# One addition of two weight slabs on VectorE is placed earlier in the order of its engine

## The reference

```
h = rmsnorm(x, g_ffn)
z = dwconv3(h @ w_up)                    # w_up: 1024 x 5632; three taps over the positions
z_gate, z_val = split(z)                 # 2816 each
x = x + (silu(z_gate) * z_val) @ w_down
```

## Time and profile before

| | |
|---|---|
| time, three runs | 1087.05, 1088.1, 1088.28 us (median 1088.1) |
| profiled execution | 1088.28 us |
| its span, first to last instruction | 1086.5 us |
| mean granted clock of TensorE | 0.996 |
| busy: PE, DVE, ACT, POOL | 1072.4, 643.6, 556.8, 629.0 us |
| `add_s2`, 16 of them | 35.1 + 12.8 us |
| POOL's `low` | 2.4 to 2.7 us each |

### The profile page before, as it was taken

One profiled execution on the slowest core, in us unless ns is written; L12 is line 12 of the kernel. 1 busy time (PEld: TensorE's weight loads), 2 busy tenths in 40 slices (PEclk: granted clock), 3 DMA queues, 4 the chain that ended last, 5 costly groups with the idle time before them and its releaser, 6 DMA issues.

```text
span 1086.5 us, 18356 instructions
## 1 busy us (share of the span) xinstructions
PE 1072.4 (99%) x6492; PEld 943.9 (87%) x6492; DVE 643.6 (59%) x938; ACT 556.8 (51%) x772; POOL 629.0 (58%) x298
## 2 busy tenths in 40 slices
PE   9999999999999999999999999999999999999997
PEld 7788888888889989998878888888879998899987
DVE  5725755667197731776636368556744786147764
ACT  7835444545356623675548244445434575257651
POOL 6334334344789848995534332434458895789940
PEclk9999999999999999999999999999999999999999
DMA  8332123232866446762522222222338763767412
GB/s 304 96 97 79 59 78 99 78 115 78 213 176 173 119 140 169 173 142 95 179 84 80 79 78 71 89 93 78 116 114 220 158 149 98 194 155 188 115 48 78
DMA packets 40549, 134.35 MB, mean 124 GB/s; under 512 B 4752, under 2 KB 7568, under 8 KB 40464
## 3 DMA queue, kind: packets, MB, share of 16 engines
q1 hardware_dynamic: 32848, 107.03, 30.5%
q0 software_dynamic: 6912, 25.17, 13.5%
q10 hardware_dynamic: 704, 1.07, 0.3%
HBM read 122.76 MB, written 2.10 MB: 115 GB/s over the span
## 4 chain that ended last, share of the span: by engine, by line
PE 95%; DVE 3%; DMA 1%; ACT 0%; POOL 0%; SPq 0%; issue 0%; DVEq 0%
PE acc L1482 18%; PE acc L1483 17%; PE acc L1484 17%; PE acc L1796 9%; PE acc L1799 9%; PE acc L1798 9%; PE acc L1608 3%; PE acc L1609 3%; PE acc L1610 3%; DVE second_s L1311 2%; PE sides L1578 1%; PE sides L1680 1%; PE sides L1696 1%; DMA x<-xT 1%; PE sides L1686 1%; PE sides L1659 1%
## 5 line engine op out<-in xcount | busy, mean ns | idle before, releaser
L465 POOL TENSOR_TENSOR w_lo<-w_raw,w_hi 128x1024 fp32r<-128x1024 f32 x108 | 261.4, 2426 | 334.9 <-ACT w_hi L522 329.0
L455 POOL TENSOR_TENSOR w_lo<-w_raw,w_hi 128x1024 fp32r<-128x1024 f32 x72 | 183.9, 2581 | 56.7 <-ACT w_hi L805 44.0
L1482 PE MATMUL acc<-feat_hi,w_hi 128*128 128x512 f32 (+1 forms) x496 | 190.1, 383 | 1.6 <-DVE x L1227 1.5
L1483 PE MATMUL acc<-feat_lo,w_hi 128*128 128x512 f32 (+1 forms) x496 | 189.7, 382 | 0.0
L1484 PE MATMUL acc<-feat_hi,w_lo 128*128 128x512 f32 (+1 forms) x496 | 189.6, 382 | 0.0
L522 ACT ACTIVATE w_hi<-w_raw 128x1024 fp32r<-128x1024 f32 x102 | 107.8, 1063 | 139.8 <-PE acc L1484 103.4
L1796 PE MATMUL acc<-xg_hi,w_hi 128*128 128x256 f32 x512 | 146.6, 286 | 4.6 <-DVE sides L1333 4.6
L1799 PE MATMUL acc<-xg_hi,w_lo 128*128 128x256 f32 x512 | 146.2, 286 | 0.0
L1798 PE MATMUL acc<-xg_lo,w_hi 128*128 128x256 f32 x512 | 146.2, 286 | 0.0
L1482 PE MATMUL acc<-xg_hi,w_hi 128*128 128x512 f32 x352 | 139.6, 397 | 0.0
L1483 PE MATMUL acc<-xg_lo,w_hi 128*128 128x512 f32 x352 | 137.1, 389 | 0.0
(11 more groups left out here) (179 smaller groups left out, 2164.6 us busy)
## 6 DMA issues: line engine op xcount, KB each, us to landing
w_raw<-slabs SPq DMA_DIRECT2D x166, 512.0 KB, 3.5
w_raw<-slabs POOLq DMA_DIRECT2D x16, 512.0 KB, 5.5
arena<-slabs SPq DMA_DIRECT2D x16, 512.0 KB, 4.8
arena<-slabs POOLq DMA_DIRECT2D x16, 512.0 KB, 5.4
mixer_sb<-slabs SPq DMA_DIRECT2D x8, 512.0 KB, 5.0
w_raw<-mixer_sb POOLq DMA_DIRECT2D x8, 512.0 KB, 4.6
mixer_sb<-second_s POOLq DMA_DIRECT2D x8, 512.0 KB, 4.5
outT<-arena SPq DMA_DIRECT2D x7, 256.0 KB, 2.2
```

Of the source, the lines that this page charges most:

```text
L455: pool.tensor_tensor(w_lo[:, w], source, w_hi[:, w].bitcast(F32), ALU.subtract).then_inc(lo_done, 1)
L465: pool.tensor_tensor(w_lo[:, w], w_raw[:, w], w_hi[:, w].bitcast(F32), ALU.subtract).then_inc(lo_done, 1)
L1482: pe.matmul(out, wh, ah, start=first, stop=False)
L1483: pe.matmul(out, wh, al, start=False, stop=False)
```

## The change

`convolve` takes a function more and calls it between the taps of tile 2 and gate 0. In quads 1 and 2 of each part that function is `add_s2(p, s + 1)`, which stood behind `convolve` and c11. In quad 0 there is no `convolve` ahead, and `add_s2(p, 1)` now stands before c11. `add_s2(p, 0)` stays where it was, and no other engine's order changes.

```diff
-                def convolve(p, s):
+                def convolve(p, s, between):
 
                     add_c12(p, s)
                     scale(p, s, 0)
...
                     taps(p, s, 2)
+                    between()
                     gate(p, s, 0)
                     taps(p, s, 3)
                     quad_low(p, s, 0)
...
                 def quad_step(p, s):
                     if s:
-                        convolve(p, s - 1)
+                        convolve(p, s - 1, (lambda: add_s2(p, s + 1)) if s < KP - 1 else (lambda: None))
+                    else:
+                        add_s2(p, 1)
                     add_c11(p, s)
-                    if s < KP - 1:
-                        add_s2(p, s + 1)
                     add_c22(p, s)
                     add_c21(p, s)
                     scale(p, s, 1)
...
-                    convolve(p, KP - 1)
+                    convolve(p, KP - 1, lambda: None)
```

## The result

The changed kernel took 1096.54 us (median of five, 1095.78 to 1098.7) against 1088.15 for the kernel before: ratio 1.0076, 95% interval 1.0057 to 1.0095. So it is slower by 8.4 us; 1097.2 was forecast, +8.9. The profiled execution took 1098.84 us with a span of 1097.0, at the upper end of what the kernel shows. Lines behind the edit are one higher than before (products are L1797, L1799, L1800). In all that follows "quad 1's add" is the add that stands in quad 1 and makes S2 for quad 2, and so on.

The account below looks back on a forecast made before the run. TensorE, busy 99% of the span, was taken as the bound, so only its stops could be won back. Two vanishing stops (-8.05) and four new ones (4.70 + 4.18 + 2 x 4.02) gave +8.9 on 1088.28: 1097.2 us, range 1087.5 to 1106.

Parts of the forecast that it names:

- The stops that vanish: Part 0's first quad, both layers: TensorE's stops of 2.69 and 2.18 us vanish, with slowed products behind them, -8.05 us.
- The rule for a waiting add: A waiting DVE add gets in only where POOL's next instruction begins later than 0.14 us before the last one's end.
- limit for the A11 low: Quads 1 and 2: A11's low must end before -0.59 us from the quad's TensorE start, or the add is held.
- the four adds of the forecast: A11's ends: part 0 quad 1 +0.34 and -0.18 (layers 0, 1), quad 2 -0.69 (served); part 1 quad 2 -0.34; others held.
- Part 1, quad 2: Add held to S4's end in both layers, TensorE 2.43 us late plus 1.59 for the clock: 4.02 us each, +8.04.
- Part 0: Quad 1's add held in both layers, costing 4.70 and 4.18 us; quad 2's served by a margin of 0.10 us, 0.
- The clock: Behind each of the four new TensorE stops a lowered clock lengthens the next product, 1.59 us each.
- The sum: Whole kernel: -8.05 + 4.70 + 4.18 + 2 x 4.02 = +8.9 us, giving 1097.2 us.
- D: Rival: all adds get in at the next low's end, in a tight chain too; 1080.2 us, chance 0.20.
- B: Rival: part 0's quad 2 add is held too, 2 x 4.0 us more; 1105.2 us, chance 0.17.
- C: Rival: only quad 1 of part 0 is held, part 1 keeps its gaps; +0.85, 1089.1 us, chance 0.18.
- E: Rival: as the forecast, but a stop of 2.4 us doesn't lower the clock; 1094.0 us, chance 0.07.

Follow-up runs that it names:

- The gap in quads 1 and 2: Changed kernel, with POOL waiting for its own A22 low before the S3 low in quads 1 and 2 only: 1080.13 us, ratio 0.9927 to the kernel before.
- a gap at the boundary: Changed kernel, with POOL waiting for its own A22 low before the S3 low in every quad: 1080.58 us, ratio 0.9939 to the kernel before.
- a gap one boundary earlier: Changed kernel, with POOL waiting for its own S2 low before the A22 low: 1081.38 us, ratio 0.9945 to the kernel before.
- no second input: Changed kernel, with the add replaced by a same-size reduction reading S1 alone (result not the layer's): 1080.56 us, ratio 0.9925 to the kernel before.
- The run with quad 0 alone: Kernel before, with only quad 0's add moved before c11, all other adds left in place: 1086.87 us, ratio 0.9993.
- The run with the gap in part 1 alone: Changed kernel, with POOL waiting for its own A22 low before the S3 low in part 1 only: 1091.54 us, ratio 1.0039 to the kernel before.

## Why the prediction was right

**The stops that vanish.** Right, both, in every execution with quad 0's move. The gap in quads 1 and 2 takes away all others, and the kernel is 7.7 us below that before where 8.05 was counted.

**The rule for a waiting add.** Right in kind, and shown by changing one thing at a time: a gap at the boundary, a gap one boundary earlier, no second input (with the operation changed along with it). An overlap of 0.12 in layer 1 let the add in, 0.34 in layer 0 did not. The number 0.14 is another matter: it is the lead with which DVE starts before a low's recorded end, and the prediction took it for the limit of the overlap too. The run with quad 0 alone served an add at 0.18, so if one limit holds for lows and DMA issues alike, it lies between 0.18 and 0.30. The forecast's limit for the A11 low, -0.59, was worked out with 0.14; with 0.18 to 0.30 it would be -0.55 to -0.43, and the four adds of the forecast (+0.34 and -0.18, -0.69, -0.34) stay on the side where they were put.

**Part 1, quad 2.** The adds and the stops are right to a few hundredths of a us. Forecast from the quad's start: A22 +6.56, S3 +8.92, S4's end +13.96, TensorE at +16.83. Measured: +6.53, +8.90, +13.97, +16.84. With the products behind them the two stops cost 5.1 us in one execution and 6.5 in the other, where 8.04 was forecast: the clock, below, makes the difference. The run with the gap in part 1 alone prices them at 4 to 5 us.

**Part 0.** Right in kind, uncertain in place. I had quad 1 held in both layers and quad 2 served, by 0.10 us. One execution shows just that; in the other, quad 2 is held in both layers and quad 1 in layer 0 only. Two causes can be read. In quad 1, layer 1, the A11 low ended at -0.31 (forecast -0.18), later than the limit of -0.59, and yet the add was served. The limit was wrong for this quad: it came from quad 3, where ACT's high for S3 is ready at +8.79, and here it was ready at +9.08, so the S3 low began only at +9.15 and A22, begun at +6.57, was just early enough. In the other execution the high was as late, but A22 began at +6.88, and the add was held. And quad 2 follows from quad 1. Where the clock stays up behind quad 1's stop, quad 2 starts sooner than the 7.35 us behind TensorE's resumption that I used (5.86, at 326.59 to 332.45), and A11's low, at +0.77, misses the limit; where quad 1 has no stop at all (layer 1) it ends at +0.42 and misses it too. So the forecast's served add in quad 2 hung on a lowered clock, which the prediction didn't say.

**The clock.** This term of the sum was mis-sized. I took 1.59 us behind each stop, four times. In the profiled executions of the changed kernel the clock fell behind two of five stops and three of four, for 1.6 to 2.8 us each. A stop of 2.77 us at 326.59 did not lower it; one of 2.18 us before the change did. What decides it stays open; it isn't the length of the stop alone.

**The sum.** Forecast for the four stops and what lies behind them: 10.56 + 6.36 = 16.9 us. One execution had five stops, 14.35 + 4.36 = 18.7; the other four, 10.7 + 6.1 = 16.8. In the first the clock's part was 2 us smaller than forecast and a fifth held add more than made up for it. In the second the clock cost 2.8, 1.6, 1.6 and 0.1 us and not 1.59 four times. That the median of five came out 0.7 us from the forecast is in part luck of this kind; which adds were held in those five executions isn't known.

**Rivals.** D (all adds served) gave 1080.2; it is what the kernel does once the chain is broken, 1080.1 to 1080.6. B, quad 2 of part 0 held, happened in one profiled execution, but not together with quad 1 in layer 1. C didn't occur. E, a clock that stays up behind stops of 2.4 us, held for both such stops in one execution and for one of two in the other; its time, 1094.0, is below every execution of the changed kernel.

## What to carry to other kernels

- Where DVE's instruction has two inputs in SBUF and POOL works through a queue, read the starts of POOL's instructions against the ends of their predecessors. Where they begin 0.3 us early, DVE may wait for the whole queue; a wait of POOL for its own last instruction opened it here (S3 then began 0.4 us later against A22's end).
- Moving a waiting instruction earlier on its engine moves the stop with it, unless it lands in a hole that exists at all its places. Quads that look alike differed by 0.8 us in POOL's lag (A11's end at -1.16 and -0.37 in quads 1 and 2 of part 1) and by 0.3 in ACT's, and that decided.
- Before an instruction is put into a chain, list every reader behind it with its due time, not only the one that is looked for: the room was 0.8 us up to S2's product, not the 3.1 between the S3 low's usual end (365.35 by the earlier trace rows, +11.28) and its product at +14.40.

## What the runs showed of the hardware

A low that comes directly behind a POOL DMA issue is recorded 0.3 us longer (2.7 for 2.4), and so are those behind it as long as none of them waits; each then begins 0.3 us before its predecessor's recorded end. A DVE addition with two SBUF inputs took up to 12.2 us beside such chains (1.22 without a wait), past the ends of four lows and a DMA issue. The Trainium skill, in the section named above, calls the shared pair of ports an exclusive lock, and says of DVE's two-port modes that whoever issues first has the pair for the whole instruction; the add at 858.05, served at the end of one low, agrees, and the held adds waited for longer than one instruction. A DVE reduction with one SBUF input took 1.22 us beside such chains.
